# Attention in groups of two pairs of heads, with the values two groups behind, in a two-model inference kernel

## What is computed

```
s = einsum('bqhgd,bkhd->bhgqk', q_blk, k) * scale      # A2, C2; masks, sinks or biases in the others
p = softmax(s, axis=-1)
out = einsum('bhgqk,bkhd->bqhgd', p, v)
# C2: q = [q_nope (64), q_rope (32)], k = [k_nope (64), k_rope (32), one for all heads]
# NSA: y = gate_0 * cmp + gate_1 * causal + gate_2 * window, then times silu(z)
```

## Time and profile before

| | before |
|---|---|
| median of 3 runs | 2277.22 us (2274.36 to 2278.72) |
| span of the profiled execution | 2275.0 us |
| PE busy | 2199.9 us, 97% |
| DVE busy | 1246.9 us, 55% |
| ACT busy | 1078.0 us, 47% |
| POOL busy | 853.7 us, 38% |
| all attention parts | about 487 us |

### The profile page before, as it was taken

One profiled execution on the slowest core, in us unless ns is written; L12 is line 12 of the kernel. 1 busy time (PEld: TensorE's weight loads), 2 busy tenths in 40 slices (PEclk: granted clock), 3 DMA queues, 4 the chain that ended last, 5 costly groups with the idle time before them and its releaser, 6 DMA issues.

```text
span 2275.0 us, 33281 instructions
## 1 busy us (share of the span) xinstructions
PE 2199.9 (97%) x12130; PEld 1763.7 (78%) x12130; DVE 1246.9 (55%) x2614; ACT 1078.0 (47%) x2160; POOL 853.7 (38%) x665
## 2 busy tenths in 40 slices
PE   8999899999999999989999999999999999999997
PEld 6778667888866788668888888888767888888886
DVE  6997782499778446885552112234666655211222
ACT  6542484465247652685453223343566545322332
POOL 4333304443330343104255545554110425554553
PEclk9999899999999999999999999999999999999998
DMA  5334002332410233203233333343110323333331
GB/s 171 85 91 141 25 2 79 104 91 79 144 38 11 75 89 109 68 2 110 67 94 96 95 109 98 92 124 95 48 60 20 111 66 97 94 95 100 98 96 66
DMA packets 107186, 189.74 MB, mean 83 GB/s; under 512 B 12049, under 2 KB 22801, under 8 KB 106897
## 3 DMA queue, kind: packets, MB, share of 16 engines
q1 hardware_dynamic: 101136, 178.67, 27.3%
q10 hardware_dynamic: 5888, 8.95, 1.2%
HBM read 182.85 MB, written 2.10 MB: 81 GB/s over the span
## 4 chain that ended last, share of the span: by engine, by line
PE 85%; DVE 10%; issue 3%; ACT 2%; POOL 1%; DMA 0%; SPq 0%; DVEq 0%; ACTq 0%
PE bank L861 23%; PE bank L863 23%; PE bank L862 23%; PE bank L1090 3%; PE bank L1103 3%; PE bank L1076 2%; DVE temp L1933 1%; DVE bank L2053 1%; PE bank L868 1%; DVE temp L1965 1%; PE bank L1067 1%; PE bank L1070 1%; PE bank L931 1%; DVE temp L1967 1%; POOL w_lo L2212 1%
## 5 line engine op out<-in xcount | busy, mean ns | idle before, releaser
L2212 POOL TENSOR_TENSOR w_lo<-w_raw,w_hi 128x512 fp32r<-128x512 f32 (+3 forms) x618 | 824.7, 1341 | 1337.1 <-ACT w_hi L1226 1336.7
L861 PE MATMUL bank<-op_hi,w_hi 128*128 128x512 f32 x1840 | 734.4, 399 | 9.1 <-POOL w_lo L2212 4.4
L863 PE MATMUL bank<-op_hi,w_lo 128*128 128x512 f32 x1840 | 719.4, 391 | 0.0
L862 PE MATMUL bank<-op_lo,w_hi 128*128 128x512 f32 x1840 | 719.4, 391 | 0.0
L1226 ACT ACTIVATE w_hi<-w_raw 128x512 fp32r<-128x512 f32 (+2 forms) x634 | 385.4, 617 | 682.5 <-PE bank L863 678.8
L861 PEld LDWEIGHTS bank<-op_hi,w_hi 128*128 128x128 f32 x1840 | 347.1, 189 | 95.7 <-issue 15.3
L862 PEld LDWEIGHTS bank<-op_lo,w_hi 128*128 128x128 f32 x1840 | 347.6, 189 | 73.4 <-issue 4.1
L863 PEld LDWEIGHTS bank<-op_hi,w_lo 128*128 128x128 f32 x1840 | 347.1, 189 | 73.7
L1648 DVE TENSOR_TENSOR temp<-bank,rstd 128x512 f32<-128x512 f32 x151 | 104.4, 691 | 396.0 <-PE bank L863 378.2
L861 PE MATMUL bank<-side_hi,w_hi 128*128 128x512 f32 (+1 forms) x628 | 233.2, 371 | 2.5 <-DVE side_lo L1730 1.4
L863 PE MATMUL bank<-side_hi,w_lo 128*128 128x512 f32 (+1 forms) x628 | 230.9, 368 | 0.0
(11 more groups left out here) (269 smaller groups left out, 2256.3 us busy)
## 6 DMA issues: line engine op xcount, KB each, us to landing
w_raw<-in_weights SPq DMA_DIRECT2D x620, 256.0 KB, 2.7
w_raw<-in_weights SPq DMA_DIRECT2D x32, 192.0 KB, 2.3
temp<-temp SPq DMA_DIRECT2D x40, 64.0 KB, 2.0
x_t<-in_x SPq DMA_DIRECT2D x8, 256.0 KB, 5.4
conv_area<-in_mem ACTq DMA_DIRECT2D x2, 1024.0 KB, 5.5
out_y<-ybuf SPq DMA_DIRECT2D x8, 256.0 KB, 2.1
conv_area<-in_bias ACTq DMA_DIRECT2D x1, 1920.0 KB, 8.0
conv_area<-in_bias ACTq DMA_DIRECT2D x2, 960.0 KB, 4.9
```

Source lines behind the costliest of these rows:

```text
L861: pe.matmul(dst, w[0], m[0], start=start, stop=False)
L862: pe.matmul(dst, w[0], m[1], start=False, stop=False)
L863: return pe.matmul(dst, w[1], m[0], start=False, stop=stop)
L2212: pool.tensor_tensor(w_lo[:, j, 0:n], w_raw[:, p % RAW_RING, 0:n], w_hi[:, j, 0:n].bitcast(F32), ALU.subtract).then_inc(*mark("weights_spl ...
```

## The change

All parts but X2 now go in groups of two pairs (four tiles); `PAIRS` says which. Step s works on whole groups. PE: scores of group s, values of group s-2, turns of group s-1. ACT: exponentials of tiles 0, 1, 2 of group s, copy of tile 0 of group s-1, exponential of tile 3, copies of tiles 1, 2, 3. DVE: for each of the two pairs, normalise that of group s-1 and take the maxima of that of group s; then the output of group s-2. All extras of the step's four moments follow at its end on every engine; those on DVE called "split" still two moments late.

Banks: scores take 1, 2, 3, 0. A group's four turns take 4, 5, the group's own output bank (in NSA 4, from tile 44 on 7) and 4 again (5 again where the third took 4). An output now holds two query blocks of a pair (256 columns); in C2 it holds two head columns at one block, and C2's tiles are ordered so that a group is two head columns at one query block: their 64-row scores are made pair by pair, then the 32-row scores of all four tiles, one in each quarter of the rows, together. NSA keeps one output bank, 6, and its layer norm moves to bank 7. `E` has eight buffers, the fourth `PT` is `rstd`, and the amounts in `DRAIN`, `GATE_CHUNKS` and `WARM_TURN` are set anew. X2 keeps its order. Cut to its core:

```diff
-TURN_LAG = 2
-VALUE_LAG = 3
-OUT_LAG = 7
+PAIRS = {"NSA": 2, "AB2": 2, "D2": 2, "C2": 2, "X2": 1}
+TURN_LAG = {1: 2, 2: 1}
+VALUE_LAG = {1: 3, 2: 2}
 LN_TILES = 44
-NORM_LAG = 3
+NEXT_SPLIT = 10
 LOW_LAG = 2
-E_RING = 6
+E_RING = 8
 PT_RING = 4
-SCORES = (1, 2, 3)
-GATE_CHUNKS = (2, 1, 1, 4)
+SCORES = (1, 2, 3, 0)
+GATE_CHUNKS = (2, 2, 4)
 WARM_END = {"NSA": 0, "AB2": 4, "D2": 1, "C2": 1, "X2": 2}
-WARM_TURN = {"NSA": {30: 3}, "AB2": {0: 1}, "D2": {0: 2}, "C2": {0: 2}, "X2": {0: 2}}
-SUMS = 24
+WARM_TURN = {"NSA": {}, "AB2": {0: 2}, "D2": {0: 2}, "C2": {0: 2}, "X2": {0: 2}}
+SUMS = 32
...
-            return bank[2 if n == 2 else 0 if n in LAST_GATE.values() else n % 2]
+            return bank[2 if n == 2 else 7 if n in LAST_GATE.values() else n % 2]
...
+                order = [(j, i) for j in range(4) for i in range(NT)]
+                if kind == "C2":
+                    order = [(j + e, i) for j in (0, 2) for i in range(NT) for e in range(2)]
+                for j, i in order:
...
+                            half, y, chunks = i % 2, ybuf[:, yc, P * (i - 1):P * (i + 1)], [yc]
+                            if kind == "C2":
+                                half, y, chunks = j % 2, ybuf[:, j - 1:j + 1, qs], [j - j % 2, j - j % 2 + 1]
                             out.append(dict(q=q, k=k, more=more, nk=nk, mask=mask, scale=scale, sink=sink, gate=None, pv=pv, cmp=False, r=r,
-                                            size=2, pos=r, width=HD, y=ybuf[:, yc, qs], chunks=[yc], qs=slice(0, P), start=True, stop=True))
+                                            size=4, pos=2 * half + r, width=HD, y=y, chunks=chunks,
+                                            qs=slice(P * half, P * half + P), start=True, stop=True))
...
-        krb = tmp(10)
+        krb = ybuf[:, 10, :]
         E = [tmp(i) for i in range(E_RING)]
-        PT = [tmp(E_RING + i) for i in range(PT_RING)]
+        PT = [tmp(E_RING), tmp(E_RING + 1), tmp(E_RING + 2), rstd[:, :]]
...
-            PROGRAM += [("split", ("mix2", l), (7,)), ("strips", ("OUT2", l)), ("strips", ("XK", l)), ("strips", ("XV", l)),
+            PROGRAM += [("split", ("mix2", l), (7,) if l == 0 else (6, 7)), ("strips", ("OUT2", l)), ("strips", ("XK", l)), ("strips", ("XV", l)),
...
-        DRAIN = {"NSA": ((), (), (0, 0), (0, 0, 1, 1, 1, 1)),
-                 "AB2": ((0, 0), (0, 0, 0), (0, 1, 1), (1, 1, 1, 1, 0, 1)),
-                 "C2": ((0, 0), (0, 0, 0), (0, 1, 1), (1, 1, 1, 1, 0, 1)),
-                 "D2": ((0,), (0,), (1,), (1,)),
+        DRAIN = {"NSA": ((), (0, 0), (), (0, 0, 1, 1, 1, 1)),
+                 "AB2": ((0, 0), (0, 0, 0, 0, 1), (), (1, 1, 1, 1, 1, 0, 1)),
+                 "C2": ((0, 0), (0, 0, 0, 0, 1), (), (1, 1, 1, 1, 1)),
+                 "D2": ((0,), (0, 1), (), (1,)),
...
-                    banks = SCORES if step[1][0] == "NSA" and at_tile - ts[0]["a"] < LN_TILES else SCORES + (0,)
-                    t["bank"] = banks[(at_tile - ts[0]["a"]) % len(banks)]
+                    n = at_tile - ts[0]["a"]
+                    t["bank"] = SCORES[n % len(SCORES)]
                     t["held"] = held.get(t["bank"])
                     held[t["bank"]] = at_tile
                     t["first"], t["last"] = t["pos"] == 0, t["pos"] == t["size"] - 1
+                    t["out"], t["out_held"] = (6, at_group - 1) if step[1][0] == "NSA" else (6 + at_group % 2, at_group - 2)
+                    t["turn"] = 4 + n % 2
+                    if PAIRS[step[1][0]] == 2:
+                        third = t["out"] if step[1][0] != "NSA" else 7 if n >= LN_TILES else 4
+                        t["turn"] = (4, 5, third, 4 if third != 4 else 5)[n % 4]
+                    t["turn_held"] = turned.get(t["turn"])
+                    turned[t["turn"]] = at_tile
...
+        def groups_of(part):
+            n = 2 * PAIRS[part[0]]
+            return [[ATT[part][i + j:i + j + 2] for j in range(0, n, 2)] for i in range(0, len(ATT[part]), n)]
+        def lags_of(part):
+            return TURN_LAG[PAIRS[part[0]]], VALUE_LAG[PAIRS[part[0]]]
+        def moments_of(part, s):
+            n = 2 * PAIRS[part[0]]
+            return range(n * s, n * s + n)
+        def steps_of(part):
+            return len(groups_of(part)) + VALUE_LAG[PAIRS[part[0]]] + 2 - PAIRS[part[0]]
+        def in_group(groups, s):
+            return groups[s] if 0 <= s < len(groups) else []
...
-                    at(18 + k, "split", ("mix2", 1), k)
-                at(32, "split", ("mix2", 1), 6)
+                    at(18 + k if k < 4 else 22 + k, "split", ("mix2", 1), k)
...
+                def free_banks(tiles_of):
+                    for t in tiles_of:
+                        if t["held"] is not None:
+                            pe.wait_ge(*after("maxed", t["held"]))
+                def latent_scores(group):
+                    parts = ((0, 0), (0, 1), (1, 0))
+                    if group[0][0]["a"] == ts[0]["a"]:
+                        pe.wait_ge(*after("rope_keys", 0))
+                    for pair in group:
+                        free_banks(pair)
+                        for x, y in parts:
+                            for t in pair:
+                                pe.matmul(score_bank(t), t["q"][x], t["k"][y], start=(x + y == 0), stop=False)
+                    for x, y in parts:
+                        for t in group[0] + group[1]:
+                            ins = pe.matmul(score_bank(t), t["more"][0][x], t["more"][1][y], start=False, stop=(x == 1))
+                            if x == 1:
+                                ins.then_inc(*mark("scores", t["a"]))
...
-                    if a >= 2:
-                        pe.wait_ge(*after("probs_copied", a - 2))
-                    warm(4 + a % 2, WARM_TURN[part[0]].get(a - ts[0]["a"], 0))
+                    if t["turn_held"] is not None:
+                        pe.wait_ge(*after("probs_copied", t["turn_held"]))
+                    if t["turn"] == t["out"] and t["out_held"] >= 0:
+                        pe.wait_ge(*after("outputs_taken", t["out_held"]))
+                    if t["turn"] == 7 and part[0] == "NSA":
+                        pe.wait_ge(*after("ln_scaled", (part[1], 3)))
+                    warm(t["turn"], WARM_TURN[part[0]].get(a - ts[0]["a"], 0))
                     pe.wait_ge(*after("probs", a))
                     for b in range(1 if t["cmp"] else len(t["pv"])):
-                        ins = pe.transpose(bank[4 + a % 2][:, P * b:P * b + P], E[a % E_RING][:, P * b:P * b + P], ident)
+                        ins = pe.transpose(bank[t["turn"]][:, P * b:P * b + P], E[a % E_RING][:, P * b:P * b + P], ident)
                     ins.then_inc(*mark("probs_turned", a))
...
+                        if t["first"] and t["out_held"] >= 0:
+                            pe.wait_ge(*after("outputs_taken", t["out_held"]))
+                        if t["first"] and t["size"] == 4:
+                            pe.wait_ge(*after("probs_copied", t["a"] + 2))
...
+                groups = groups_of(part)
+                turn_lag, value_lag = lags_of(part)
+                for s in range(steps_of(part)):
+                    if part[0] == "C2" and s < len(groups):
+                        latent_scores(groups[s])
+                    else:
+                        for pair in in_group(groups, s):
+                            scores(pair)
+                    if part[0] == "NSA" and s + 1 < len(GATE_CHUNKS):
+                        for _ in range(GATE_CHUNKS[s + 1]):
+                            next(begun[LAST_GATE[part[1]]])
+                    if 0 <= s - len(groups) < 3:
+                        drain(part, steps[s - len(groups)])
+                    if PAIRS[part[0]] == 2:
+                        for pair in in_group(groups, s - value_lag):
+                            values(pair)
+                    for pair in in_group(groups, s - turn_lag):
+                        for t in pair:
+                            turn(t)
+                    if PAIRS[part[0]] == 1:
+                        for pair in in_group(groups, s - value_lag):
+                            values(pair)
+                    for i in moments_of(part, s):
+                        for stage in between.get(i, ()):
+                            extra_stage(*stage)
...
+                groups = groups_of(part)
+                turn_lag, _ = lags_of(part)
+                for s in range(steps_of(part)):
+                    if NEXT_SPLIT in moments_of(part, s):
                         split_to(last_of(FOLLOWS[part] + 1))
-                    if 2 * TURN_LAG <= i < len(ts) + 2 * TURN_LAG:
-                        copy(ts[i - 2 * TURN_LAG])
-                    if i < len(ts):
-                        exps(ts[i])
-                    for stage in between.get(i, ()):
-                        extra_stage(*stage)
+                    to_exp = [t for pair in in_group(groups, s) for t in pair]
```

(66 more changed lines are left out.)

75 lines of the change are left out of this document (19 added, 56 removed).

## The result

The changed kernel takes 2365.56 us (median of 4 runs, 2364.46 to 2368.69) against 2277.19 (4 runs, 2274.36 to 2278.72). The ratio is 1.0389, with a 95% interval of 1.0374 to 1.0404. Its profiled execution has a span of 2362.7 us (before 2275.0). The forecast was 2313 in a range of 2255 to 2335: the direction was right, the size was not, and the time lies outside the range.

The account below looks back on a forecast made before the run. PE was taken to bound, with DVE and ACT nearly balanced and DVE bounding AB2's windowed half. NSA +14.6, AB2 +17, D2 +3.7, C2 +0.9 and cross attention 0 gave +36 us on 2277.2: 2313, range 2255 to 2335.

Parts of the forecast that it names:

- the chain of the late turn: Ordinary steps: PE's fourth turn waits for ACT's copy of tile 0; D2 and AB2 steps 5.92 us, C2 7.5.
- The bias: D2: the bias load is issued late and DVE's scales wait for it; two steps of 8.7 us, net +2.9.
- the sign named for it: D2's bias: the changed profile would show DVE idle ahead of the bias scale, released by the DMA.
- The rival in which the queues don't stop PE: Copies, lows and scales come early enough, PE gives 19 us back where it bounds: 2258 us, chance 0.20.
- the four-wide pass: C2's 32-row scores: a pass of four products takes 0.23 us, like a two-wide one.
- the splits: AB2 and C2: DVE's low waits for ACT's high behind the copies; AB2 split steps 8.5 us, AB2 +17 in all.
- the step that priced the clock: Rival: PE's clock falls in new gaps of AB2, D2 and C2, 17 us more, 2330 us, chance 0.10.
- the term of NSA: Both NSA layers: chain interpolated for tiles of 128 to 512 columns; +7.3 us a layer, +14.6 together.
- the missing third bank: NSA up to tile 44: no third turn bank, so tile 3 waits for the copy of tile 1, behind exponential 3.
- the layer norm's factor: NSA's second head column: PE waits 4.2 us for it, behind ACT's copies, where it was 3.3 before.
- The end: End of NSA: PE waits some 6.7 us for last values behind ACT's copies and SiLUs, now 2.7; +2.3 net.
- PE's work of 5.4: A group of D2 or AB2's first half needs 5.4 us of PE, 0.5 less through fewer changes of kind.

Follow-up runs that it names:

- e13: Changed kernel plus idle products only where PE stands idle (two per step after a low in AB2, eight at each NSA end): 2355.6 us.
- e3: Changed kernel with DVE's low part of a split one step later than ACT's high: 2334.1 us.
- e10: Changed kernel with a third turn bank (bank 7) for three more groups of NSA: 2355.6 us.
- e8: Changed kernel with NSA by pairs; in AB2, D2 and C2 low one step later and copy after two exponentials; D2's bias loaded one step earlier: 2274.7 us.
- e7: e6 with C2's 32-row products ordered by pairs: 2316.7 us.
- e11: Changed kernel, groups everywhere, with e3, e4 (not in NSA), earlier bias, e10 and three idle products at NSA's tile 30: 2314.4 us.
- e14: Changed kernel with PE spreading the layer norm's factor one step later and DVE scaling later: 2368.4 us.
- e5: Changed kernel with turned tiles on two banks everywhere, no third bank: 2405.9 us.
- e1: Changed kernel plus two idle products ahead of the first turn of every step of NSA and AB2: 2391.1 us.
- e4: Changed kernel with ACT's first copy after two exponentials of a step, not three: 2350.7 us.
- e6: Changed kernel with e3 and e4 together: 2318.8 us.
- e9: e8 plus the three idle products that the kernel before had ahead of NSA's turn of tile 30: 2270.8 us.
- e12: e6 with C2 going head column by head column, so both pairs use the same two quarters of the rows: 2320.0 us.
- e2: Changed kernel with NSA alone back to steps of one pair, with its drain: 2313.5 us.

## Why the prediction was wrong

**Right: the chain of the late turn.** D2's and AB2's step 5.88 (forecast 5.92), C2's 7.47 (7.5). D2 in all is +4.0 (+3.7), but that is luck. The bias was put at +2.9, with two steps of 8.7; they took 7.7 and 7.0, which is 2.9 over two ordinary ones and only 0.3 over what the bias cost before. DVE waited 0.3 us for the load in all, so the sign named for it didn't show. Longer steps elsewhere (two of 6.7, the start and the end, 0.8 to 1.1 each) made it up. The rival in which the queues don't stop PE is refuted by the waits above, and the four-wide pass costs 0.23 us as taken. The figure of the Trainium skill ("TensorE: Matmul & The Clock Gate", section "Measured speedup vs the span model"), weighed in the part on latent scores, made it 0.30. The trace doesn't agree: twelve products take 0.90, what the six of a pair took in the earlier trace rows.

**Right in mechanism and size, at full clock: the splits.** The forecast had AB2 at +17, with split steps of 8.5. At a clock of 1.00 (e13) AB2 is +18.4 and the steps are 8.55. Moving the low (e3) takes 15.1 of it back.

**Wrong: the step that priced the clock.** It was a rival with 0.10, and it was an addition, not an alternative. It gave AB2, D2 and C2 17 us and NSA, where the clock was known to be low already, nothing. Measured: AB2 6.7 (e13 against the changed kernel) and C2 2.7 (e10 and e13, with the same instructions). For NSA an estimate: PE's busy time went from 100.4 and 100.9 us, less 2.8 for the three products that are gone, to 104.7 and 107.1, +7 and +9. In pairs such time is paid nearly in full (e8); in groups, where PE waits more, less. The two layers of one kernel have the same instructions, and over the ten kernels with NSA in groups in which their busy times differ by a microsecond or more (the changed one, e3 to e7, e11 to e14) the longer layer is always the one with more busy time: 24.9 us more in sum, and 16.3 in length, two thirds. So NSA paid some 11 to 16 us, and the three parts together 20 to 25 of the 52 missed. The rival's 17 us was not far off, its places were.

**Wrong: the term of NSA.** Forecast +7.3 a layer, of which 2.3 at the end; measured 26, some 18 to 21 without the clock. I interpolated the chain of D2 for tiles of different width and took the missing third bank as a small correction. The waits for copies are the largest item, from 3.2 to 16.5 us. e5 prices the bank at about 1 us a step, e10 at 0.4 to 0.8; for 11 groups that is 4 to 11 us a layer, an estimate. By head column (a group of two columns counted half to each) the first NSA took 28.4, 37.1, 29.9 and 41.8 us; the forecast had 25.3, 29.9, 27 and, with the end, 35.9. So most was missed in the second column, where the tiles have two turn banks throughout and the layer norm's factor comes (its wait is 3.1 us, 4.2 were forecast), and at the end. The end waits 6.9 us as forecast (6.7), but the tail from the start of the last group is 23.1, not 19.1. ACT has four exponentials and eight copies there ahead of the SiLUs, and the last 32 values run partly at 1.2 GHz. The single output bank (3.1) was not in the forecast at all. Both layers together grew by 52.5 us; without their 11 to 16 of the clock and the 14.6 forecast, 22 to 27 are left, and with the clock's 25 to 20 in all parts that makes 47 of the 52 missed. The rest is C2 (+3.1 at a clock of 0.98 for +0.9: its steps 2 and 3 take 8.9 us, not 7.5), AB2's 1.4 and 0.8 between the attentions.

**Right in size, but never free: PE's work of 5.4.** e1's step shows 5.35. But with the late turn gone (e4) the step was 5.83: the values wait for the copy of the third tile, a second wait that the forecast hadn't seen behind the first.

The range failed although its upper end, 2335, had room for both: 7.3 us for one and a half times NSA and 17 for the clock (2337 by that sum). NSA's true factor was two and a half to three, and the clock cost more, in NSA above all.

**Still open.** How NSA's 18 to 21 us divide between the bank, the mixed widths and the output bank, and how much of its loss is the clock (no run brought the clock of NSA in groups up without adding work where PE doesn't wait): three turn banks from the start weren't tried, since the layer norm and the score tiles hold the others. Nor is it settled why e4 lengthens NSA, and why e6 doesn't.

## What to carry to other kernels

When a kernel is regrouped, write out for one step what stands ahead of each handoff on each engine; here that gave the ordinary steps to 0.05 us. Do it for each kind of step (two banks, mixed widths, the end) and don't interpolate, and then add the price of TensorE's lower clock wherever the new gaps stand, also where it was low before. Larger groups paid (e9) only where three turn banks were free, the copy came early and each low stood a step behind its high, and then by little but for C2's four-wide products. And read what a filler product costs from start to start, with all its instructions, before it is put in.

## What the runs showed of the hardware

Products in four different quarters of 32 rows start four at a time even if the kernel gives first three passes for two quarters and then three for the others (e7: starts 1771.67, 1772.01, 1772.24, each for four); in the same two quarters the same twelve take 1.60 us, not 0.91 (e12). The Trainium skill, "TensorE: Matmul & The Clock Gate", section "The mechanism", says that matmuls start and end strictly in the order of the program. This trace shows otherwise for the starts.

The granted clock of one and the same instruction stream differs between stretches and kernels: 0.84 and 0.92 (e8, two layers), 0.86, 0.89 and 0.93 (AB2 in the changed kernel, e2 and e10), worth 7.7 us in e8 and 4.1 from 0.86 to 0.93. It differs between executions of one kernel too: 0.980 to 0.989 over the whole of e8, worth 15 us. Twelve more idle products in AB2, two in each of six gaps, held it at 1.00 (e13).
